# A hybrid encoder layer on one Trainium2 core: attention's product with the values as one 32-bit matmul in place of three rounded ones

## What is computed

```python
logits = (jnp.einsum('bhqd,bhkd->bhqk', q[:, :, lo:hi], k[:, :, :hi]).astype(jnp.float32) * scale
          + cum[:, :, lo:hi, None] - cum[:, :, None, :hi])
logits = jnp.where(s_pos[None, :] <= t_pos[:, None], logits, -jnp.inf)
p = jax.nn.softmax(logits, axis=-1)
outs.append(jnp.einsum('bhqk,bhkd->bhqd', p.astype(v.dtype), v[:, :, :hi]))
...
y_b = o_b.reshape(b, s, FOX_WIDTH) * jax.nn.silu(z_b)
```

## Time and profile before

| | |
|---|---|
| Time, median of 3 runs (lowest, highest) | 1598.03 us (1595.36, 1600.0) |
| Span of the profiled execution | 1594.5 us |
| PE busy over the span | 1544.6 us (97%), 7890 matmul records |
| DVE, ACT, POOL busy | 929.7 (58%), 691.0 (43%), 628.4 us (39%) |
| Stage `mix` in the trace | first matmul at 819.05 us, first one of `project_out` at 1408.15 us |

### The profile page before, as it was taken

The page is one execution under the profiler, slowest core; times in us unless marked ns, Lnnn a source line. Parts: engine busy times, 40 slices in busy tenths (PEclk is TensorE's granted clock), DMA queues, the critical chain, the costliest instruction groups (busy, mean ns, idle before and its releaser), DMA issues. The chain is left out here.

```text
span 1594.5 us, 22173 instructions
## 1 busy us (share of the span) xinstructions
PE 1544.6 (97%) x7890; PEld 1225.9 (77%) x7890; DVE 929.7 (58%) x1436; ACT 691.0 (43%) x1307; POOL 628.4 (39%) x540
## 2 busy tenths in 40 slices
PE   7999999999999999999989999998999999989998
PEld 5888888888888888888856776776677767767886
DVE  7455555555416766910237686676578676645755
ACT  0346364544511111131116676766677777831100
POOL 2212121221211111101126787877797888921111
PEclk9999999999999999999979999999999999999999
DMA  6134335261583333227535646463546465324642
GB/s 256 46 116 134 111 101 144 73 172 60 152 138 123 128 119 103 90 80 152 158 107 151 164 120 179 137 152 96 148 126 165 132 161 166 93 77 125 196 134 92
DMA packets 190657, 206.49 MB, mean 129 GB/s; under 512 B 50940, under 2 KB 134140, under 8 KB 187516
## 3 DMA queue, kind: packets, MB, share of 16 engines
q1 hardware_dynamic: 189972, 203.24, 44.9%
q10 hardware_dynamic: 576, 1.84, 0.3%
HBM read 129.79 MB, written 75.17 MB: 129 GB/s over the span
## 5 line engine op out<-in xcount | busy, mean ns | idle before, releaser
L1510 POOL TENSOR_TENSOR m_p_lo<-m_p,m_p_hi 128x512 fp32r<-128x512 f32 (+1 forms) x320 | 374.9, 1192 | 68.1 <-ACT m_p_hi L1474 64.8
L554 PE MATMUL bank<-x_hi,w_hi 128*128 128x512 f32 x992 | 394.2, 397 | 0.0
L554 PE MATMUL bank<-x_hi,w_lo 128*128 128x512 f32 x992 | 387.1, 390 | 0.0
L554 PE MATMUL bank<-x_lo,w_hi 128*128 128x512 f32 x992 | 386.2, 389 | 0.0
L579 POOL TENSOR_TENSOR w_lo<-w_raw,w_hi 128x512 fp32r<-128x512 f32 x64 | 92.8, 1472 | 481.1 <-ACT w_hi L638 481.1
L1472 ACT ACTIVATE m_p<-m_st,fcol 128x512 f32<-128x512 f32 (+1 forms) x320 | 203.9, 637 | 147.2 <-PE m_st L1352 70.9
L1562 DVE TENSOR_REDUCE m_maxima<-m_aux 128x1 f32<-128x512 f32 (+2 forms) x320 | 193.4, 618 | 107.5 <-PE m_aux L1327 63.5
L554 PEld LDWEIGHTS bank<-x_hi,w_lo 128*128 128x128 f32 x992 | 186.2, 188 | 40.2
L554 PEld LDWEIGHTS bank<-x_lo,w_hi 128*128 128x128 f32 x992 | 186.6, 188 | 36.2
L554 PEld LDWEIGHTS bank<-x_hi,w_hi 128*128 128x128 f32 x992 | 186.5, 188 | 36.0
L1474 ACT ACTIVATE m_p_hi<-m_st,fcol 128x512 fp32r<-128x512 f32 (+1 forms) x320 | 202.1, 632 | 0.0
(11 more groups left out here) (214 smaller groups left out, 2533.9 us busy)
## 6 DMA issues: line engine op xcount, KB each, us to landing
w_raw<-in_w SPq DMA_DIRECT2D x31, 512.0 KB, 3.8
dram_feat<-ring SPq DMA_DIRECT2D x48, 256.0 KB, 4.2
arena<-dram_gates SPq DMA_DIRECT2D x32, 256.0 KB, 4.8
o_y<-dram_mixT SPq DMA_DIRECT2D x16, 512.0 KB, 6.2
o_x<-in_x SPq DMA_DIRECT2D x16, 512.0 KB, 4.1
out<-o_res SPq DMA_DIRECT2D x15, 512.0 KB, 5.0
arena<-in_xT SPq DMA_DIRECT2D x7, 1024.0 KB, 9.5
K<-dram_k_hi SPq DMA_DIRECT2D x12, 512.0 KB, 8.0
```

The source lines that it names most:

```text
L554: mm = pe.matmul(banks[bank_of(s)][:], w[:, i % 2, k * P:(k + 1) * P], x[:, k, b * BLOCK:(b + 1) * BLOCK], start=(k == 0 and n == 0), stop ...
L1510: pool.tensor_tensor(p_lo[(s - 1) % PL][:, off:], p[(s - 1) % PL][:, off:], p_hi[(s - 1) % PH][:, off:].bitcast(F32), ALU.subtract).then_i ...
```

## The change

The rounded and the low parts of the probabilities and of the values go. ACT takes one exponential for each unit, in float32; POOL's subtraction is gone; PE has one matmul for each unit on float32 operands, `v` (with the column of ones) by `p`. `p` has six places. DVE copies the values once and subtracts nothing. A pad keeps other tiles where they were.

```diff
-ST, PH, PL = 2, 4, 3
+ST, PL = 2, 6
...
-                    done(pe, p_hi_ready, s - ST)
+                    done(pe, p_ready, s - ST)
...
-                    pe.wait_ge(p_hi_ready, s + 1)
-                    pe.matmul(b[0:FD + 1, off:], v_hi[i % 2][:, kb, j, :], p_hi[s % PH][:, off:], start=kb == 0, stop=False)
-                    pe.matmul(b[0:FD, off:], v_lo[i % 2][:, kb, j, :], p_hi[s % PH][:, off:], start=False, stop=False)
-                    pe.wait_ge(p_lo_ready, s + 1)
-                    pe.matmul(b[0:FD + 1, off:], v_hi[i % 2][:, kb, j, :], p_lo[s % PL][:, off:], start=False,
+                    pe.wait_ge(p_ready, s + 1)
+                    pe.matmul(b[0:FD + 1, off:], v[i % 2][:, kb, j, :], p[s % PL][:, off:], start=kb == 0,
                               stop=kb == 4 * g + 3).then_inc(pv_done, 1)
...
-                    done(act, p_lo_ready, s - PL)
+                    done(act, pv_done, s - PL)
                     act.activation(p[s % PL][:, off:], st[s % ST][:, off:], ACT.Exp, bias=bias).then_inc(p_ready, 1)
-                    done(act, pv_done, s - PH)
-                    act.activation(p_hi[s % PH][:, off:], st[s % ST][:, off:], ACT.Exp, bias=bias).then_inc(p_hi_ready, 1)
...
-                    if 0 <= s - 1 < N_UNITS:
-                        off = unit(s - 1)[3]
-                        done(pool, pv_done, s - 1 - PL)
-                        pool.wait_ge(p_hi_ready, s)
-                        pool.tensor_tensor(p_lo[(s - 1) % PL][:, off:], p[(s - 1) % PL][:, off:],
-                                           p_hi[(s - 1) % PH][:, off:].bitcast(F32), ALU.subtract).then_inc(p_lo_ready, 1)
...
-                        dve.tensor_copy(v_hi[i % 2][:, cut, :, 0:FD], src).then_inc(v_hi_ready, 1)
-                        dve.wait_ge(v_hi_ready, 4 * i + blk + 1)
-                        dve.tensor_tensor(v_lo[i % 2][:, cut, :, :], src, v_hi[i % 2][:, cut, :, 0:FD].bitcast(F32), ALU.subtract)\
-                           .then_inc(v_ready, 1)
+                        dve.tensor_copy(v[i % 2][:, cut, :, 0:FD], src).then_inc(v_ready, 1)
```

More of the change, by code:

```diff
@@ L1085, in mix @@
             scr["o_y"] = [ahead.enter_context(nc.sbuf_tensor(f"o_y{i}", [P, KT, P], F32)) for i in range(4)]
-        v_lo, v_hi = ([scr["shared"].enter_context(nc.sbuf_tensor(f"m_{n}0", [P, NCH, 2, w], F32R))]
-                      for n, w in (("v_lo", FD), ("v_hi", FD + 1)))
+        v = [scr["shared"].enter_context(nc.sbuf_tensor("m_v0", [P, NCH, 2, FD + 1], F32))]
+        scr["shared"].enter_context(nc.sbuf_tensor("y_pad", [P, NCH, 2, FD], F32))
         scr["o_y_lo"] = [scr["shared"].enter_context(nc.sbuf_tensor("o_y_lo0", [P, KT, P], F32R))]
@@ L1104, in mix @@
         v_feat = home["v_feat"]
-        v_hi.append(sb("v_hi1", [P, NCH, 2, FD + 1], F32R))
-        v_lo.append(sb("v_lo1", [P, NCH, 2, FD], F32R))
+        v.append(sb("v1", [P, NCH, 2, FD + 1]))
         p = [sb(f"p{i}", [P, 512]) for i in range(PL)]
-        p_hi = [sb(f"p_hi{i}", [P, 512], F32R) for i in range(PH)]
-        p_lo = [sb(f"p_lo{i}", [P, 512], F32R) for i in range(PL)]
         maxima = sb("maxima", [P, 4, 4])
@@ L1137, in mix @@
         yb_stored = scr["yb_stored"] = [nc.alloc_semaphore(name=f"yb_stored{i}") for i in range(2)]
[L1138 to L1143, removed]
+        (v_landed, aux_ready, aux_used, v_ready, mcol_ready, max_diag_ready, row_ready,
+         scores_ready, p_ready, pv_done, den_ready, gated_ready, yb_ready) = (sem(n) for n in (
+             "v_landed", "aux_ready", "aux_used", "v_ready", "mcol_ready", "max_diag_ready", "row_ready",
+             "scores_ready", "p_ready", "pv_done", "den_ready", "gated_ready", "yb_ready"))
         norm_landed, half_w_ready, S_zeroed, XT_zeroed = (sem(n) for n in (
@@ L1479, in _ @@
                 for i in range(2):
-                    pool.memset(v_hi[i][:, :, :, FD:].bitcast(F32), 1.0)
+                    pool.memset(v[i][:, :, :, FD:], 1.0)
                 pool.memset(half[:], -0.5)
```

## The result

The changed kernel takes 1611.33 us (median of 4 runs, 1610.81 to 1614.93) against 1597.16 us before in the same series: a ratio of 1.0102 with a 95% interval of 1.0077 to 1.0128. By the ratio that is 16 us slower (12 to 20), by the two medians 14 us; the forecast was 37 us. The ratio is an estimate of its own, with its interval, and not the quotient of the medians, so a difference can read 2 us larger or smaller with the choice. A later series gave 1613.59 us and 1.0101 (1.0080 to 1.0122). The profiled execution took 1611.46 us with a span of 1609.6 us.

What follows compares the result with a forecast made beforehand. PE was taken as the bound, busy 520.58 of 538 us. PE's +53 us less 16 us of waits gave +37, a span of 1631.5 us; with 3.5 us carried over, 1635 us, range 1608 to 1660.

Steps and rivals of the forecast that it cites:

- Part 1: PE work that goes: three fp32r products a unit, 0.70, 0.52 or 0.35 us by columns, 196 us in all.
- Part 2: PE work that comes: one float32 matmul a unit, two records of 0.445 us at 512 columns, net +53 us.
- low bound: Least net PE cost of the float32 matmuls: exactly two periods a column and nothing beside it, 43 us.
- change-over: Extra 0.08 us on PE before the next product starts; up to 26 us if each of 320 units pays it.
- four passes: Skill's count for a true 32-bit product on PE; at the fp32r price 0.92 us a unit, 63 us in all.
- rival of cheap columns: 512 columns cost PE only 0.23 us a float32 record, so the kernel gets faster, 1526 us; chance 0.08.
- Part 3: POOL's 374.9 us of subtractions go; worth only PE's ended waits and some clock, -16 us (bounds -8 and -32).
- Part 4: ACT loses 202.1 us of exponentials, worth nothing; DVE loses 11.1 us: nothing, or part of PE's 6.4 us waits.
- second rival: Waits eat the price: PE's price near 43 us, nearly all waits go (-32), 1609 us or less; chance 0.07.
- third rival: The clock falls: PE gets 1.2 GHz more often during float32 records, 71 us more, 1706 us; chance 0.05.
- The signs: Expected profile: 320 fewer PE records, ACT near 203 and POOL near 90 us busy, a stage of some 626 us.

## Why the prediction came out too high

By its own steps:

- **The bound was right.** PE sets the stage before and after, and the time moved the way that was forecast. `project` and `project_out` did not change (819.05 and 818.52 us up to the stage, 186.4 and 186.5 us behind it).
- **Part 1 was right**: 0.70, 0.52 and 0.35 us a unit.
- **Part 2 was mis-sized by 7 to 10 us.** A record of 512 columns costs 0.43 us, not the 0.445 scaled up from the chain's short ones, so the term is 46 us by single rows and 43 to 44 by slots, not 53; the "low bound", two periods a column and nothing beside it (43 us), was nearly exact. A short record's 0.111 us for 128 columns is more than two periods a column (0.107), so scaling it up overstates. The change-over of 0.08 us a unit does not exist here: the price by slots would hold it. The Trainium skill's four passes ("FP8 and Floating Point Precision", "TensorE Precision Notes") are borne out in columns: 0.86 us is 2064 periods at 2.4 GHz, four for each of 512. My price for them, 0.92, charged each pass what a whole fp32r record costs. The rival of cheap columns was wrong.
- **Part 3 failed, and with Part 4 it is the step that decided.** I put the waits that end at 16 us; 28 to 30 us ended. The three terms that I gave for POOL (8.0 for `p_lo`, 4.5 for the diagonal, a choice of 4 for the clock; 16.5 us) measure 11 us when the subtraction goes together with the second exponential, and of the diagonal's 4.5 us nearly all stayed (4.2). That the waits in the view of PE fell by 16 us in all is a coincidence: 5.1 of them are DVE's. What was missing is the effect of the longer unit: Part 4 has "nothing, or a part of the 6.4 us" for DVE, because I asked what DVE loses in work (11.1 us) and not what it gains in time by a longer unit. The run with padding alone shows that 12 of 45 us come back with nothing else changed; the fp32r kernel without the subtraction and with the padding among the values gives back 45 - 19 = 26 us, nearly what the changed kernel does.
- **The two effects are not separate parts of a sum.** 11 us (subtraction gone) and 12 (padding) come near to the 20 us that come back in the kernel with both edits and the padding in the same place (45 - 25). But that is luck, as the 33 slots show that hold the give-back. In 14 of them, 13.5 us in the changed kernel, each edit alone already gives back most: 12.0 us without the subtraction, 9.6 with the padding. Those waits end when either the awaited result comes sooner or PE comes later. Seven more come back with one edit alone. In the other 12, 8.8 us, neither edit alone gives back anything (3.4 us of it at the slots of the reciprocal above, 1144 and 1150 us), and what they need was not found: both edits together with the padding among the values give back 2.5 of the 8.8 us, and a second profile of the changed kernel has 6.8.
- **The second rival describes it best**: "the price is near 43 us and nearly all of the waits go". I gave it 0.07, for times up to 1608 us, because it took both bounds at once. The measured 1611 us lies just inside the range of the forecast, near its low end, and it got there by the rival's way: a price at the low bound and 28 to 30 of the 32 us of waits. A smaller price should have given back less and not more, so nothing tied the two together, and my doubt of both at once was fair by what I knew; what I lacked was the slack.
- **The lower clock** went with the waits: 0.98 to 1.00 over the same window. The third rival was wrong.
- **The signs**: PE has 7570 records, 320 fewer; POOL is busy for 91 us in the stage (90 forecast); the stage has 604.6 us and not 626. ACT is busy for 242 us and not 203: one exponential's 202.1 us can't be subtracted from the windows' 405, since records of ACT overlap (the two groups of exponentials sum to 406.0 us, more than all of ACT's busy time in those windows).

What stays open: which chains make up the 8.8 us that neither edit alone gives back, and the 3 us of the padding's place. The reciprocal's DMA is one place, shown by moving it; but moving it ended no time, since the next wait (queries for maxima, or the diagonal) took its place.

The experiments found faster kernels only by leaving work out: two products on rounded probabilities take 3.0% less than before, one takes 3.5% less (4.0% with the later reciprocals). Of the kernels that compute all parts none is faster than the kernel before.

## What to carry to other kernels

When an edit makes the bounding engine's slot longer or shorter in a schedule that is counted in slots, don't carry the waits of the old trace over as a constant: everything with a length in microseconds (a DMA, a reduction that another engine must deliver) gets more or less of the slot. Here a slot longer by 0.16 us gave back over a quarter of its own price, while slots shorter by 0.23 and again 0.23 us yielded 38 and 10 of 65 us each. Nor should savings of two edits be added: either may end the same wait. A single wait taken out of such a schedule tends to surface at the next step, so test it before counting it. Price an unseen long matmul by clock periods for its columns, not by scaling a short one's start-to-start time.

## What the runs showed of the hardware

- A float32 product of 512 columns shows as two records and costs 0.86 us, of 384 columns 0.65, of 256 columns 0.44; the fp32r one 0.23, 0.17 and 0.12. So three fp32r products (0.70) are cheaper than one float32 product (0.86), at 64 or 65 columns of weights and a granted clock of 1.00.
- DVE's operations on SBUF are slower while POOL's float32 subtraction on SBUF runs: `m_on` takes 1302 ns in the kernel before, 694 in the changed one and 724 in the one before without the subtraction, and 1051 in the changed one with a lighter subtraction on POOL (973 ns in place of 1192).
- Where PE waits longer the granted clock of the stretch is lower: 1.00, 0.99, 0.96 and 0.90 in the table above, from the least waits to the most.
